# HGRN level products of a head in one run behind chunk 8, with buffers of their own

## The reference, cut to what matters

```python
h = rms_norm(x) * (1 + scale) + shift
proj = h @ w_in          # 2048 x 9216: rq, rk, rv, rg, hq, hf_f, hf_b, hi, hg; 8 heads of 128 each
# group A, retention, and group B, HGRN2, each forward and backward in time
f = lb + (1 - lb) * sigmoid(z);  log_f = log(f);  k = 1 - f
b = cumsum(log_f)                                # within a chunk
scores = einsum('bhid,bhjd,bhijd->bhij', q, k, exp(b_i - b_j))   # j <= i
o = scores @ v + (q * exp(b)) @ s
s = exp(b_last) * s + (k * exp(b_last - b)).T @ v
o_h = rms_norm(o_f + o_b) * silu(hg)
out = concat(o_r, o_h) @ w_out
x = x + gate * out;  y = rms_norm(x)
```

## Time and profile before

| | us |
|---|---|
| median of three runs (lowest, highest) | 1402.61 (1402.18, 1403.21) |
| profiled execution, own time | 1402.38 |
| its span, first to last instruction | 1400.6 |
| TensorE busy with matmuls | 1383.8 (99%) |
| VectorE busy | 999.3 (71%) |
| ScalarE busy | 483.7 (35%) |
| GpSimd busy | 368.1 (26%) |

### The profile page before, as it was taken

One profiled execution on the slowest core, in us unless ns is written; L12 is line 12 of the kernel. 1 busy time (PEld: TensorE's weight loads), 2 busy tenths in 40 slices (PEclk: granted clock), 3 DMA queues, 4 the chain that ended last, 5 costly groups with the idle time before them and its releaser, 6 DMA issues.

```text
span 1400.6 us, 24702 instructions
## 1 busy us (share of the span) xinstructions
PE 1383.8 (99%) x10042; PEld 1165.8 (83%) x10042; DVE 999.3 (71%) x1330; ACT 483.7 (35%) x842; POOL 368.1 (26%) x292
## 2 busy tenths in 40 slices
PE   7999999999999999999999999999999999999997
PEld 5788898889888988898889888988898888888886
DVE  5555676667689889988898889877676768532345
ACT  4323243234333333342334333333333344221234
POOL 0000114311532153215321532153206225201220
PEclk9999999999999999999999999999999999999999
DMA  9994442435343535454444454433443357182235
GB/s 387 418 418 161 117 126 69 120 72 139 95 161 108 172 94 178 111 153 119 161 116 140 128 166 114 130 97 106 106 106 86 103 151 278 53 305 93 90 106 210
DMA packets 207735, 212.40 MB, mean 152 GB/s; under 512 B 144256, under 2 KB 156816, under 8 KB 202768
## 3 DMA queue, kind: packets, MB, share of 16 engines
q1 hardware_dynamic: 207600, 210.89, 47.9%
q10 hardware_dynamic: 32, 0.02, 0.0%
HBM read 182.27 MB, written 24.40 MB: 148 GB/s over the span
## 4 chain that ended last, share of the span: by engine, by line
PE 95%; DMA 3%; DVE 1%; SPq 0%; issue 0%; ACT 0%; DVEq 0%; ACTq 0%
PE ps L2122 10%; PE ps L2124 10%; PE ps L2123 10%; PE ps L1957 9%; PE ps L1958 8%; PE ps L1959 8%; PE ps L1933 8%; PE ps L2299 5%; PE ps L2301 5%; PE ps L2300 5%; DMA area<-in_w_mod 2%; PE ps L2139 2%; PE ps L1964 2%; PE ps L1965 2%; PE ps L1966 2%; PE ps L1923 2%
## 5 line engine op out<-in xcount | busy, mean ns | idle before, releaser
L1201 DVE TENSOR_TENSOR w_lo<-area,w_hi 128x1024 fp32r<-128x1024 f32 x143 | 190.3, 1331 | 206.7 <-ACT w_hi L729 206.7
L729 ACT ACTIVATE w_hi<-area 128x1024 fp32r<-128x1024 f32 x143 | 151.5, 1059 | 495.5 <-PE ps L2124 266.1
L2122 PE MATMUL ps<-w_hi,hT_hi 128*128 128x512 f32 x640 | 251.1, 392 | 0.0
L2124 PE MATMUL ps<-w_hi,hT_lo 128*128 128x512 f32 x640 | 249.1, 389 | 0.0
L2123 PE MATMUL ps<-w_lo,hT_hi 128*128 128x512 f32 x640 | 249.0, 389 | 0.0
L1957 PE MATMUL ps<-hT_hi,w_hi 128*128 128x512 f32 x512 | 204.8, 400 | 0.0
L1958 PE MATMUL ps<-hT_lo,w_hi 128*128 128x512 f32 x512 | 199.7, 390 | 0.0
L1959 PE MATMUL ps<-hT_hi,w_lo 128*128 128x512 f32 x512 | 199.6, 390 | 0.0
L2124 PEld LDWEIGHTS ps<-w_hi,hT_lo 128*128 128x128 f32 x640 | 120.1, 188 | 25.2
L2122 PEld LDWEIGHTS ps<-w_hi,hT_hi 128*128 128x128 f32 x640 | 120.2, 188 | 24.3
L2123 PEld LDWEIGHTS ps<-w_lo,hT_hi 128*128 128x128 f32 x640 | 120.2, 188 | 24.1
(11 more groups left out here) (282 smaller groups left out, 2427.7 us busy)
## 6 DMA issues: line engine op xcount, KB each, us to landing
area<-in_w_in SPq DMA_DIRECT2D x144, 512.0 KB, 4.2
area<-in_w_mod SPq DMA_DIRECT2D x26, 1024.0 KB, 12.3
area<-in_w_out SPq DMA_DIRECT2D x38, 512.0 KB, 3.9
gate_raw<-in_w_gate SPq DMA_DIRECT2D x32, 512.0 KB, 4.0
gate_raw<-in_w_mod SPq DMA_DIRECT2D x6, 1024.0 KB, 12.1
o_hi_scratch<-area SPq DMA_DIRECT2D x56, 80.0 KB, 2.4
o_lo_scratch<-area SPq DMA_DIRECT2D x56, 80.0 KB, 2.4
hT_hi<-o_hi_scratch SPq DMA_DIRECT2D x14, 320.0 KB, 7.0
```

What stands on the lines that cost most here:

```text
L729: act.activation(split_weights(h, n)[0], raw[:, n % 3, :], ACT.Copy).then_inc(wt_hi.sem, 1)
L1201: v.tensor_tensor(lo, raw[:, n % 3, :], hi.bitcast(F32), ALU.subtract).then_inc(wt_lo.sem, 1)
L2122: mm(out, hT_hi[:, k, tile_cols(t)], w_hi[:, n % 2, w], start=k == 0, stop=False)
L2124: i = mm(out, hT_lo[:, k, tile_cols(t)], w_hi[:, n % 2, w], start=False, stop=k == KT - 1)
```

## The change

- Every level gets operand buffers of its own while the head before is in work (`decayed`: the halves of `XE`, `KL`, parts of the retention's buffers; level 6 uses `sT` and `kl_tokens`). `differences` of levels 1 to 6 then wait for `pe_hu` (the key updates behind chunk 1), not for scores.
- Differences stand at items 3 (level 1), 4 (2, 3), 5 (4, 5) and 6 (6); exponentials and decays at items 4 (level 1), 5 (2, 3), 6 (4, 5) and 7 (6). The sum of the keys is made behind level 6, into K.
- All eight products run behind chunk 8 (`all_scores`), the diagonal last. The gate reduction stays behind chunk 5.
- Scores of levels 2 to 6 are packed, 32 columns a tile, in banks C and DD. `place_all` at item 9 has two copies and five masked copies of 640 columns.
- Work of the next head that writes buffers now in longer use waits for `pe_level`; the retention's first states are loaded at item 14.
- The last head keeps its old order; only its `key_sum` moves behind the level-0 differences.

```diff
+DIFFERENCES = {3: (1,), 4: (2, 3), 5: (4, 5), 6: (6,)}
+DECAYS = {4: (1,), 5: (2, 3), 6: (4, 5), 7: (6,)}
+SCORED = 8
+PACKED, PACK = 2, TILES * QUAD
...
+        decayed = {0: XE[:, 0], 1: KL, 2: XE[:, 1], 3: halves(area[:, RET1:RET1 + 2 * T]),
+                   4: halves(area[:, KTL0:KTL0 + 2 * T]), 5: halves(area[:, KTL0 + 2 * T:KTL0 + 4 * T])}
...
+        def level_queries(following, level):
...
             if following is None:
+                return XE[:, level % 2, 0, :]
+            return decayed[level][:, 0, :] if level in decayed else sT
...
-                if n == 6 and h is not None:
+                if n == 14 and h is not None:
...
-            def differences(h, level):
+            def differences(h, following, level):
...
-                if due(pe_level, h, level):
+                if following is not None and level:
+                    dve.wait_ge(pe_hu.sem, pe_hu.at(h))
+                elif due(pe_level, h, level):
...
+            def place_all(h):
+
+                dve.wait_ge(pe_level.sem, pe_level.at(h))
+                v.tensor_copy(tiles(hsT[:, P:T]), tiles(ps[:, A, :])).then_inc(h_sT.sem, 1)
+                v.tensor_copy(hsT[:, 0:P], ps[:, DD, 0:P]).then_inc(h_sT.sem, 1)
+                quads = hsT.rearrange("p (t b n) -> p t b n", t=TILES, n=QUAD)
+                for level in range(PACKED, LEVELS):
...
+                    v.copy_predicated(quads, where, scores).then_inc(h_sT.sem, 1)
...
-                    if n == 4:
-                        place(prev, h, 0)
-                    if n in (4, 6, 8):
-                        differences(prev, n - 3)
-                        differences(prev, n - 2)
...
-                    if 4 <= n < 3 + LEVELS:
-                        own_decay(prev, n - 3)
+                    for level in DIFFERENCES.get(n, ()):
+                        differences(prev, h, level)
+                    for level in DECAYS.get(n, ()):
+                        own_decay(prev, h, level)
+                    if n == SCORED + 1:
+                        place_all(prev)
...
-                    if n in (4, 6, 8):
-                        differences(prev, n - 3)
-                        differences(prev, n - 2)
-                        key_decay(prev, n - 3)
-                        key_decay(prev, n - 2)
+                    for level in DIFFERENCES.get(n, ()):
+                        differences(prev, h, level)
+                    for level in DECAYS.get(n, ()):
+                        key_decay(prev, h, level)
+                    if n == SCORED - 1:
+                        pool.wait_ge(la.sem, la.at(prev, LEVELS))
+                        key_sum(prev, K[:, 0, :])
...
+            def packed_tile_scores(out, keys, queries):
+
+                for c_ in range(4):
+                    rows = slice(c_ * QUAD, (c_ + 1) * QUAD)
+                    i = mm(out[rows], keys[:, rows], queries[:, rows], start=True, stop=True)
+                return i
+
+            def all_scores(h, following):
...
+                for level in range(LEVELS):
+                    pe.wait_ge(la.sem, la.at(h, level + 1))
+                    pe.wait_ge(lq.sem, lq.at(h, level + 1))
...
-                    if n == 3:
-                        level_scores(prev, h, 0)
-                        level_scores(prev, h, 1)
-                    if n in (5, 7, 9):
-                        level_scores(prev, h, n - 3)
-                        if n == 5 and 0 <= gate_block(prev) < GATE_BLOCKS:
-                            gate_reduced(prev)
-                        level_scores(prev, h, n - 2)
+                    if n == 5 and 0 <= gate_block(prev) < GATE_BLOCKS:
+                        gate_reduced(prev)
+                    if n == SCORED:
+                        all_scores(prev, h)
```

More of the change, by code:

```diff
@@ L381, in out_bank, with ctx_scores, level_keys, packed_scores @@
             return ((0, 1, 2, 3, BB), (A, C, DD, 0, 1))[nb % 2][t]
-        def ctx_scores(following, product):
+        def ctx_scores(product):
+            return ps[:, BB if product <= 2 else DD, 0:P]
+        def level_queries(following, level):
             if following is None:
[L386 to L391, removed]
+                return XE[:, level % 2, 0, :]
+            return decayed[level][:, 0, :] if level in decayed else sT
+        def level_keys(following, level):
+            if following is None:
+                return XE[:, level % 2, 1, :]
+            return decayed[level][:, 1, :] if level in decayed else kl_tokens[:, 8 * P - T:]
+        def packed_scores(level):
+            i = level - PACKED
+            return ps[:, C, i * PACK:(i + 1) * PACK] if i < 3 else ps[:, DD, P + (i - 3) * PACK:P + (i - 2) * PACK]
         def query_chunk(h):
@@ L959, in items @@
                     context_columns(h)
-                if prev is not None and n in (4, 6, 8):
-                    decays(prev, n - 3)
-                    decays(prev, n - 2)
+                if prev is not None:
+                    for level in DECAYS.get(n, ()):
+                        decays(prev, h, level)
                 if n == 11:
@@ L1032, in _ @@
             items(CHUNKS - 1, last, None)
-            decays(last, 0)
+            decays(last, None, 0)
             tokens_context(last)
@@ L1673, in _ @@
             hgrn_silu(last, 0)
-            place(last, None, 3)
-            differences(last, 4)
+            place(last, 3)
+            differences(last, None, 4)
             hgrn_silu(last, 1)
@@ L1691, in _ @@
             hgrn_silu(last, 3)
-            place(last, None, 7)
+            place(last, 7)
             hgrn_silu(last, 4)
@@ L1822, in differences @@
                 pool.wait_ge(h_scan.sem, h_scan.at(h))
-                if due(pe_level, h, level):
+                if following is not None and level:
+                    pool.wait_ge(pe_hu.sem, pe_hu.at(h))
+                elif due(pe_level, h, level):
                     pool.wait_ge(pe_level.sem, pe_level.at(h, level))
@@ L1873, in items @@
                         pool.wait_ge(a_used.sem, a_used.at(ADA_CHUNKS - 1))
-                    key_sum(h)
-                    differences(h, 0)
+                    differences(h, None, 0)
             def head(h, prev):
@@ L1885, in _ @@
             last = HEADS - 1
-            key_decay(last, 0)
+            key_sum(last, XE[:, 1, 1, :])
+            key_decay(last, None, 0)
             key_factors(last)
             for level in range(1, LEVELS):
-                differences(last, level)
-                key_decay(last, level)
+                differences(last, None, level)
+                key_decay(last, None, level)
             pool.wait_ge(fnw_in.sem, fnw_in.at(0))
@@ L2337, in _ @@
             first_block(2, 0)
-            level_scores(last, None, 3)
+            level_scores(last, 3)
             first_block(2, 1)
```

217 lines of the change are left out of this document (114 added, 103 removed).

## The result

The changed kernel takes 1443.24 us (median of 4 runs, 1441.96 to 1444.38), the kernel before beside it 1402.39 (4 runs): ratio 1.0291, 95% interval 1.0278 to 1.0304. The forecast was 1407.1 us, with a range from 1397.3 to 1412.0. Slower was forecast and slower it is, but by luck: the loss that the forecast had counted, at chunk 7, did not come, and one that it had put at nothing did.

What follows compares the result with a forecast made beforehand. TensorE was taken to bound the kernel (95% of the chain of waits). To 1402.61 us, heads 3 to 6 add 1.8 each (+7.2) and heads 1, 2, 7 save 0.9 each (-2.7): +4.5, 1407.1 us; range 1397.3 to 1412.0.

Steps and rivals of the forecast that it cites:

- I take nothing lost: The one run of 320 score matmuls behind chunk 8 keeps its pace; bound 1.4 us a head.
- long run slower, or idle costs the clock: Rival: the long score run is paced slower (9.8 us more, 1416.9), or idling costs TensorE its clock, same size; 4%.
- The saving by switches: Entering and leaving a score run costs 0.30 us; fewer runs in heads 1 to 7 take off 5.1 us.
- The gate reduction alone: Behind chunk 5, the gate reduction as its own run on TensorE takes 0.70 us.
- w_lo of chunk 7 2.4 us late in four heads: VectorE delivers w_lo late, so TensorE idles 2.4 us before chunk 7 in heads 3 to 6.
- the same sum: The no-stall rival: w_lo 7 in time, the runs' 5.1 us come off 1402.61, giving 1397.5 us; 24%.
- My frame: VectorE's timeline in a head with gate steps: these end at 639.1, w_lo 7 at 659.3, due 656.9.
- the 16 instructions: VectorE's queue from the gate steps to the end of w_lo 7 takes 20.2 us; under 17.8 means no stall.
- One instruction each: VectorE and GpSimd take turns between items 3 and 7, stretching w_lo from 1.18 to 1.82 us.
- No wait at the run: GpSimd finishes key sum and level 6 before the scores' run starts at 672.9; no wait.
- nothing from the placement, the stores, KL and context edges: Placing behind w_lo 10, state loads at item 14, and ScalarE's KL and context copies cost nothing in total.

Runs made afterwards that it cites:

- four-run kernel: Changed kernel with its products in four runs, two behind each of chunks 5, 6, 7 and 8, gate reduction inside the first; 1402.9 us.
- kernel of three runs: Changed kernel with its products in three runs: two behind chunk 5, three behind chunk 7, three behind chunk 8; 1400.21 us.
- aligned kernel: Changed kernel with two runs of four products, behind chunks 6 and 8, plus 330 unread semaphore increments in TensorE's program; 1399.37 us.
- run of 240 records: Changed kernel with two products behind chunk 5 and the other six in one run behind chunk 8; 1423.24 us.
- the wide ones: Changed kernel with the packed matmuls of levels 2 to 6 moving 128 columns instead of 32; 1434.36 us.

## Why the prediction was wrong

- **"I take nothing lost" for the pace of a run of 320 records: the step that failed.** The earlier trace rows looked for slower records late in 80. The pace does not sink in a run; it stops, once the held instructions are used up, and 80 records are too few to show it. I bounded it by 1.4 us a head "slower"; it cost 4.7 us a head in gaps, and 1.9 more in low clock behind them, 46.0 us in all.
- **The clock.** I argued against it with the earlier trace rows, where TensorE was busy 3.69 of 6.50 us in many small pieces. The rival "long run slower, or idle costs the clock" had the right place at 4% and the wrong size, 9.8 us instead of 46.0.
- **The saving by switches** (5.1 us) was of the right size: 0.25 to 0.38 us each in the kernels without gaps. Seven of the 17 can be had safely, 14 with the runs placed by hand; all 17, in one run of 320, cost more than they bring.
- **The gate reduction alone** took 667.94 - 666.49 - 0.68 = 0.77 us, forecast 0.70:

```profile
666.49 0.39 PE L1998 MATMUL ps<-w_hi,hT_lo 128*128 128x512 f32 x1
666.81 0.64 PE L2108 MATMUL ps<-gate_sums,con 128*32 128x256 f32 x8
...
667.94 0.39 PE L1991 MATMUL ps<-hT_hi,w_lo 128*128 128x512 f32 x1
```

- **w_lo of chunk 7 2.4 us late in four heads: wrong.** This stall, 9.6 us over the four heads, was the whole reason for forecasting slower. With none, the same sum gives 1397.5 us, faster than before. In head 4 that w_lo ended at 672.31, and chunk 7 was due at 674.3: 2.0 us early. My frame fits up to the gate steps (w_lo 5 starts at 656.42, in the forecast's frame 639.1, 17.3 us shifted), but the 16 instructions took 15.9 us, not 20.2. VectorE, then GpSimd, in that stretch:

```profile
656.42 1.22 DVE L1226 TENSOR_TENSOR w_lo<-area,w_hi 128x1024 fp32r<-128x1024 f32 x1
657.55 0.48 DVE L1486 TENSOR_TENSOR area<-area 128x320 f32<-128x320 f32 x1
...
659.16 0.81 DVE L1346 TENSOR_TENSOR area<-area 128x640 f32<-128x640 f32 x1
...
670.43 1.88 DVE L1226 TENSOR_TENSOR w_lo<-area,w_hi 128x1024 fp32r<-128x1024 f32 x1
```
```profile
656.25 5.21 POOL L1868 TENSOR_TENSOR area<-area 128x320 f32<-128x320 f32 x1 [11.46 <-ACT area L899]
661.41 1.86 POOL L1869 TENSOR_TENSOR area<-area 128x320 f32<-128x320 f32 x1
```

  From 656.4 to 660.7 seven VectorE instructions ran back to back at about their lone durations, and one key decay of GpSimd, 0.87 alone, lasted 5.21, to 0.75 us after the last of them. "One instruction each" does not hold in this stretch: GpSimd got its turn when VectorE paused. Behind it both are stretched again, as forecast. The four-run kernel, with the same VectorE and GpSimd work and no loss, bears out that this contention costs TensorE nothing.
- **No wait at the run, nothing from the placement, the stores, KL and context edges:** right; none is among TensorE's waits.

## What to carry to other kernels

Count instructions, not only microseconds: the instruction row of the DMA queues and an engine's record count give the records in one fetched packet (127 here), and a stretch of short instructions longer than that can meet two packet ends and stop for 2 to 5 us. Keep such runs below one packet, as the kernel of three runs does (1400.21 us); more than that (the aligned kernel, 1399.37) hangs on the program's layout: increments put in ahead of a run move its gaps or take them away, and so may any other edit there. A wait "for nothing that the profile shows", at places that move from one repetition to the next, is the sign of it. Idle time of TensorE can cost more than itself through the clock: 6 us cost 2.5 more, 2.07 us among large matmuls nothing more.

## What the runs showed of the hardware

- Instruction packets come later while data are moving. The stretch from the run's start to about its first or only gap, heads 1 to 7 of the changed kernel (us, PE busy, clock, DMA share, GB/s):

```profile
254.80:257.00 2.20, 2.20 (x194) 1.00 0.04 7
399.20:401.70 2.50, 2.50 (x219) 1.00 0.64 180
544.20:546.70 2.50, 2.50 (x235) 1.00 0.98 341
688.00:690.70 2.70, 2.70 (x250) 1.00 0.92 317
831.80:834.70 2.90, 2.90 (x265) 1.00 0.89 318
976.70:979.00 2.30, 1.95 (x158) 1.00 0.03 7
1120.60:1123.00 2.40, 2.16 (x182) 1.00 0.04 7
```

  The gaps behind them are 2.16, 4.74, 4.43, 4.61, 4.11, 2.12 and 2.32 us: about 2.2 where the DMA engines stood still, 4.1 to 4.7 where weights were loading. The run of 240 records repeats it: 4.98, 4.80 and 3.85 us at shares of 1.0, 1.76, 2.39 and 2.54 at 0.00 to 0.04. The packets of all 38 gaps tell where the time goes: they start 0.8 to 1.7 us behind the packet end before where no data moved, 1.3 to 2.0 us where a load had just begun, 2.6 to 4.2 us where weights were loading throughout, and take 0.9 to 1.5 us either way. No run varied the loads alone, so that the data hold the packet back is argued from this, if without exception.
- The Trainium skill (Trainium Architecture — The Big Picture, The software stack) has the instruction streams brought into each engine when a program is loaded. The q8 row, with 79 packets inside the measured execution, shows TensorE's still coming in while the program runs; where the two differ, the measurement decides.
- TensorE's clock fell to the 1.2 GHz level behind every gap of 3.7 us or more, behind none of 2.07 us between large matmuls, behind none of the 1.1 to 2.2 us at the wide ones, and behind some of 1.9 to 2.9 us beside short ones. What decides between these is open.
- A first packet end within some 13 records of a run's start cost nothing at the second (seven runs): the packet that belongs to it had started 1.0 to 2.9 us before TensorE got there. Behind an end 20 records in, it started 0.8 us after, and there was a gap. So TensorE asks some way ahead of what it executes; no run measured how many instructions.
